# Feed-forward input projections computed by feature, weights as the stationary operand

## The chip, the core and the metric

The kernel runs on one core of a Trainium2 chip. The metric is the device time of the whole launch in microseconds (us). One core has a matrix engine (TensorE, PE in the rows; its weight loads are shown apart as PEld), a vector engine (VectorE, DVE), a scalar engine (ScalarE, ACT), GpSimd (POOL) and a queue engine (SyncE, SP) that issues DMAs. TensorE multiplies a stationary operand of up to 128 x 128 numbers, loaded by a weight load, with a moving operand of up to 512 columns, and adds the result into PSUM. PSUM has eight banks of 512 float32 numbers for each of 128 partitions.

## The reference

Two decoder layers run over 256 tokens of width 2048. Layer 0 mixes tokens by two attention families, layer 1 by a state-space scan. Each layer then has the same feed-forward part, on which the change bears:

```
h = layernorm(alpha * h + mix)
ple = (p[i] @ ple_w[i]) * sigmoid(h @ ple_gate_w[i])
g, u = split(h @ ffn_w_in[i], 2)          # 2048 -> 2 x 5632
h = layernorm(alpha * h + (silu(g) * u) @ ffn_w_out[i] + ple)
```

All is float32. The input projection has 2 x 5632 output features, the output projection maps 5632 features back to 2048.

## The kernel before, in words

**Number format.** Each float32 operand of a large product is split in two numbers of the type float32r, a high part and the rest: `WH` and `WL` for weights (tiles w_hi, w_lo), `XH` and `XL` for activations (x_hi, x_lo), `HH` and `HL` for the hidden features (hid_hi, hid_lo). A product is three matmuls: high with high, high with low, low with high. Activations stand with features on partitions: `XH[:, kt, :]` holds 128 features of all 256 tokens.

**Chunks.** Weights stream in chunks of 256 rows by 512 columns (512 KB). A chunk passes through a ring of four slots: SP loads it to `RAW`, ACT writes `WH` (L712), DVE writes `WL` (L999), TensorE uses both and then counts up `w_used`, which frees the slot. `chunk` (L354 to L364) does one chunk: for each of its two row tiles and each of the two token tiles (128 tokens), three matmuls with the activations stationary (128 x 128) and 512 weight columns moving (L360, L361, L362). That is 12 matmuls of 512 columns and 12 weight loads. The result has tokens on partitions.

**Blocks.** A block is 512 output columns; two PSUM accumulators, each of two banks, alternate between blocks. An input projection block of the feed-forward part takes eight chunks. Its 512 columns are 256 gate features and the 256 matching up features. The hidden width is worked in part A (12 blocks) and part B (10 blocks); after each part comes the output projection over its features (outA with 4 blocks of 12 chunks, outB with 4 blocks of 10 chunks). In both layers together the input projections have 44 blocks, so 352 chunks. The blocks between the first and the last of a part are run by a hardware loop whose body holds two blocks: five passes in part A and four in part B. The function `blocks` writes this loop.

**From accumulator to hidden operand.** While TensorE works on block k, the result of block k-1 is finished. ACT applies Silu to the gate half of both token tiles (`silu`, L877, into `GT[:, 0]`). DVE multiplies by the up half (`hidden`, L1288, into `GT[:, 1]`) and frees the accumulator. TensorE transposes the product (`hidden_turn` calls `turn`, four transposes of 128 x 128, L376) after its fourth chunk of block k, since the output projection needs features on partitions. ACT writes the high part from the transposed PSUM tile (`hidden_hi`, L717) and DVE the rest (`hidden_lo`, L1007). The last block of each part is turned within the first output block.

**What sets the order.** Nothing is scheduled automatically: each engine has its own instruction list, written out in program order, and semaphores with counts tie them (`hid_ready`, `turn_done`, `turned`, `acc_free`, `w_used`, `lo_ready`). `TG` and `HG` number the groups of transposes.

One other place is of use for comparison: the rope key projection (L423 to L425, 48 matmuls) already has weights stationary, 64 columns of them, and 256 token columns moving.

Of the kernel before, what the change touches and what calls it, by code (L numbers as in the profile page):

```python
# [18 lines left out]
F32 = mybir.dt.float32  # L19
F32R = mybir.dt.float32r  # L20
I32 = mybir.dt.int32
ALU = mybir.AluOpType
ACT = mybir.ActivationFunctionType
AX_X = mybir.AxisListType.X

P = 128
# [38 lines left out]
def lin(const, coef=0, i=None):  # L65

    return const if i is None else i * coef + const
# [15 lines left out]
def build(nc, t, out):  # L83
# [3 lines left out]
    with ExitStack() as ctx:  # L87
# [3 lines left out]
        def sem(name):  # L91
            return ctx.enter_context(nc.semaphore(name))
# [105 lines left out]
        ln_act, ln_pool = sem("ln_act"), sem("ln_pool")  # L198

        ple_ready, gate_act, silu_done, hid_ready = sem("ple_ready"), sem("gate_act"), sem("silu_done"), sem("hid_ready")  # L200
        glu_step = sem("glu_step")
        tab, tab_ready, coef_out, ab_turned, ab_ready = sem("tab"), sem("tab_ready"), sem("coef_out"), sem("ab_turned"), sem("ab_ready")
        e_raw = [sem("e_raw0"), sem("e_raw1")]
# [12 lines left out]
        TG = {}  # L216
        n = 0
        for name, count in [("x", 8), ("p0", 1), ("lat", 4), ("qk", 8), ("kpe", 1), ("qn", 4), ("qp", 2), ("kn", 4),
                            ("ln10", 8), ("hid0", FA + FB), ("p1", 1), ("ln11", 8),
                            ("hid1", FA + FB)]:  # L220
            TG[name] = n
            n += count

        HG = {}
        n = 0
        for name, count in [("x", 8), ("p0", 1), ("lat", 4), ("ln10", 8), ("hid0", FA + FB), ("p1", 1), ("ln11", 8),
                            ("hid1", FA + FB)]:
            HG[name] = n
            n += count

# [120 lines left out]
        def _(pe):  # L351
            def chunk(c, coef, i, hi, lo, kt, depth, acc, width=WB):

                pe.wait_ge(lo_ready, lin(c + 1, coef, i))  # L354
                s = c % RING
                for k in range(2):
                    for q in range(TT):
                        cols = slice(q * P, (q + 1) * P)
                        o = A[:, acc, q, 0:width]
                        pe.matmul(o, hi[:, kt + k, cols], WH[:, s, k, 0:width], start=(kt + k == 0), stop=False)  # L360
                        pe.matmul(o, hi[:, kt + k, cols], WL[:, s, k, 0:width], start=False, stop=False)  # L361
                        last = pe.matmul(o, lo[:, kt + k, cols], WH[:, s, k, 0:width], start=False,  # L362
                                         stop=(kt + k == depth - 1))
                last.then_inc(w_used, 1)  # L364

            def acc_ready(b, coef=0, i=None):
# [3 lines left out]
            def turn(g, src, col, coef=0, i=None):  # L370

                if g >= 2:
                    pe.wait_ge(turned, lin(g - 1, coef, i))
                for k in range(2):
                    for q in range(TT):
                        last = pe.transpose(TP[:, g % 2, k, q * P:(q + 1) * P],  # L376
                                            src[:, q, col + k * P:col + (k + 1) * P], ID[:])
                last.then_inc(turn_done, 1)
# [149 lines left out]
            def feed_forward(layer):  # L528
# [46 lines left out]
                            last = pe.matmul(o, BT[:, a, ri, :], CO[:, ri, a, 0:SUB, :], start=(ri == 0), stop=(ri == 1))  # L575
                    last.then_inc(k_done, 1)

                def hidden_turn(b, coef=0, i=None):

                    done = (FA + FB) * layer + b  # L580
                    pe.wait_ge(hid_ready, lin(done + 1, coef, i))
                    turn(TG[f"hid{layer}"] + b, GT[:, 1], 0, coef, i)

                for part, n_in, first in (("A", FA, 0), ("B", FB, FA)):
                    _, per, c0, b0 = PHASES[f"in{part}{layer}"]

                    def inner(k, i):
                        acc_ready(b0 + k, 2, i)
                        for j in range(per):
                            chunk(c0 + per * k + j, 2 * per, i, XH, XL, 2 * j, KT, (b0 + k) % 2)  # L590
                            if j == 3 and k > 0:
                                hidden_turn(first + k - 1, 2, i)
                        if layer == 0 and part == "B" and k == n_in - 1:
                            response(4)
                    blocks(pe, n_in, inner)
                    _, per, c0, b0 = PHASES[f"out{part}{layer}"]
                    for b in range(4):
                        acc_ready(b0 + b)
                        for j in range(per):
                            if b == 0 and j == per - 1:  # L600
                                pe.wait_ge(turned, TG[f"hid{layer}"] + first + n_in)
                            elif b == 0 and j == 0:
                                pe.wait_ge(turned, TG[f"hid{layer}"] + first + n_in - 1)
                            chunk(c0 + per * b + j, 0, None, HH, HL, 2 * j, 2 * n_in, (b0 + b) % 2)
                            if b == 0 and j == 3:
                                hidden_turn(first + n_in - 1)
                        if layer == 0 and (part == "A" or b < 3):
                            response(b if part == "A" else 5 + b)

# [86 lines left out]
        def _(act):  # L696
# [140 lines left out]
            def feed_forward(layer):  # L837
# [31 lines left out]
                def silu(b, coef=0, i=None):  # L869

                    part, k = ("A", b) if b < FA else ("B", b - FA)
                    end(f"in{part}{layer}", k, coef, i)
                    done = (FA + FB) * layer + b
                    if done:
                        act.wait_ge(hid_ready, lin(done, coef, i))
                    parity = (PHASES[f"in{part}{layer}"][3] + k) % 2
                    act.activation(GT[:, 0], A[:, parity, :, 0:256], ACT.Silu).then_inc(silu_done, 1)  # L877

                def hidden_hi(b, coef=0, i=None):
                    k = b if b < FA else b - FA  # L880
                    hi_turned(TG[f"hid{layer}"] + b, HH[:, bass.ds(lin(2 * k, 2 * coef, i), 2), :], coef, i)

                for part, n_in, first in (("A", FA, 0), ("B", FB, FA)):
                    _, per, c0, _ = PHASES[f"in{part}{layer}"]
# [99 lines left out]
        def _(dve):  # L984
# [259 lines left out]
            def feed_forward(layer):  # L1244
# [37 lines left out]
                def hidden(b, coef=0, i=None):  # L1282
                    part, k = ("A", b) if b < FA else ("B", b - FA)
                    bb = PHASES[f"in{part}{layer}"][3] + k
                    done = (FA + FB) * layer + b
                    dve.wait_ge(silu_done, lin(done + 1, coef, i))
                    dve.wait_ge(turn_done, lin(TG[f"hid{layer}"] + b, coef, i))
                    dve.tensor_tensor(GT[:, 1], A[:, bb % 2, :, 256:512], GT[:, 0],  # L1288
                                      ALU.mult).then_inc(hid_ready, 1)

                def hidden_free(b, coef=0, i=None):
                    part, k = ("A", b) if b < FA else ("B", b - FA)
# [4 lines left out]
                def hidden_lo(b, coef=0, i=None):  # L1297
                    k = b if b < FA else b - FA
                    rows = bass.ds(lin(2 * k, 2 * coef, i), 2)
                    lo_turned(TG[f"hid{layer}"] + b, HG[f"hid{layer}"] + b, HH[:, rows, :],  # L1300
                              HL[:, rows, :], coef, i)

                def out_end(part, b, stats):
                    bb = PHASES[f"out{part}{layer}"][3] + b
# [739 lines left out]
```

## Time and profile before

| | |
|---|---|
| median of three runs | 2391.46 us (2389.5 to 2392.58) |
| profiled execution, its own time | 2393.34 us |
| its span, first to last instruction | 2391.5 us |
| mean granted TensorE clock | 0.988 of full speed |
| PE busy | 2316.9 us, 97% of the span |
| PEld busy | 1918.7 us, 80% |
| DVE, ACT, POOL busy | 1450.1, 1022.3, 201.7 us |
| DMA | 478.47 MB, mean 200 GB/s |

The span is what the rows cover; about 1.8 us of the execution's own time lie around it. Busy time counts a matmul from start to modelled end. Matmuls are pipelined, so the mean duration of one (about 390 ns for 512 columns) is longer than the distance to the next start, and it is the distance between starts that tells the rate. A weight load has a row of its own and may run beside the matmul before it.

### The profile page before, as it was taken

The page shows a single profiled execution, that of the slowest core. Times are in us where ns is not written, and L with a number is a line of the kernel's source. Part 1 is how long each engine was busy: PE and PEld are TensorE (multiplying, and loading weights), DVE is VectorE, ACT ScalarE, POOL GpSimd, SP SyncE. Part 2 cuts the span into 40 slices and gives each one's busy share as a digit, 9 for nine tenths or more (in the row PEclk, how much of TensorE's full clock was granted, in tenths as well). Part 3 has the DMA queues.
Part 4 walks back from the last instruction along what each step waited for, and adds up shares of the span by engine and source line. Part 5 has one row for each costly group of instructions (what it writes and reads, how often), then busy time and mean ns, then how long its engine had stood idle before and what let it go on. Part 6 is the DMA issues. An engine that isn't in the chain of part 4 may idle for free.

```text
span 2391.5 us, 34755 instructions
## 1 busy us (share of the span) xinstructions
PE 2316.9 (97%) x12283; PEld 1918.7 (80%) x12283; DVE 1450.1 (61%) x1831; ACT 1022.3 (43%) x1136; POOL 201.7 (8%) x312
## 2 busy tenths in 40 slices
PE   8999999999999999999997799999999999999996
PEld 7888788788888888888886688778888888888885
DVE  5545757666666776556868656665545444545455
ACT  4443544444444334444341544444454433444432
POOL 0000048601111111000100000000000000000000
PEclk9999999999999999999998999999999999999998
DMA  6555254768878777666865356566555555555563
GB/s 235 183 183 160 85 197 156 223 217 263 263 254 259 243 234 237 216 223 205 281 214 177 113 192 190 180 221 194 192 185 192 186 192 193 194 185 192 186 193 114
DMA packets 133881, 478.47 MB, mean 200 GB/s; under 512 B 16144, under 2 KB 17712, under 8 KB 132624
## 3 DMA queue, kind: packets, MB, share of 16 engines
q1 hardware_dynamic: 119280, 427.35, 54.6%
q0 software_dynamic: 13216, 48.20, 6.2%
q8 instruction: 72, 1.18, 0.2%
q10 hardware_dynamic: 1280, 1.48, 0.2%
q14 instruction: 33, 0.27, 0.0%
HBM read 457.82 MB, written 19.14 MB: 199 GB/s over the span
## 4 chain that ended last, share of the span: by engine, by line
PE 94%; DVE 3%; issue 1%; DMA 1%; ACT 1%; SPq 0%; DVEq 0%; ACTq 0%
PE ps L360 29%; PE ps L362 29%; PE ps L361 29%; PE ps L376 1%; PE ps L651 1%; PE ps L664 1%; PE ps L675 1%; DMA raw<-in_w_in 1%; PE ps L386 1%; DVE w_lo L999 0%; PE ps L503 0%; PE ps L575 0%; PE ps L486 0%; PE ps L485 0%; DVE res L1229 0%
## 5 line engine op out<-in xcount | busy, mean ns | idle before, releaser
L999 DVE TENSOR_TENSOR w_lo<-raw,w_hi 128x1024 fp32r<-128x1024 f32 x775 | 951.0, 1230 | 838.3 <-ACT w_hi L712 835.2
L712 ACT ACTIVATE w_hi<-raw 128x1024 fp32r<-128x1024 f32 x775 | 820.5, 1060 | 1165.0 <-PE ps L362 1137.3
L360 PE MATMUL ps<-w_hi,x_hi 128*128 128x512 f32 x2304 | 903.6, 392 | 10.8 <-DVE x_lo L1007 7.2
L362 PE MATMUL ps<-w_hi,x_lo 128*128 128x512 f32 x2304 | 898.0, 390 | 0.0
L361 PE MATMUL ps<-w_lo,x_hi 128*128 128x512 f32 x2304 | 897.4, 390 | 0.0
L360 PEld LDWEIGHTS ps<-w_hi,x_hi 128*128 128x128 f32 x2304 | 432.9, 188 | 101.7 <-DVE x_lo L1007 9.1
L362 PEld LDWEIGHTS ps<-w_hi,x_lo 128*128 128x128 f32 x2304 | 432.9, 188 | 90.8
L361 PEld LDWEIGHTS ps<-w_lo,x_hi 128*128 128x128 f32 x2304 | 433.1, 188 | 88.1
L360 PE MATMUL ps<-w_hi,hid_hi 128*128 128x512 f32 x704 | 275.2, 391 | 0.0
L361 PE MATMUL ps<-w_lo,hid_hi 128*128 128x512 f32 x704 | 274.1, 389 | 0.0
L362 PE MATMUL ps<-w_hi,hid_lo 128*128 128x512 f32 x704 | 273.9, 389 | 0.0
L360 PEld LDWEIGHTS ps<-w_hi,hid_hi 128*128 128x128 f32 x704 | 132.1, 188 | 28.5 <-issue 1.4
L362 PEld LDWEIGHTS ps<-w_hi,hid_lo 128*128 128x128 f32 x704 | 132.2, 188 | 27.7
L361 PEld LDWEIGHTS ps<-w_lo,hid_hi 128*128 128x128 f32 x704 | 132.2, 188 | 27.2
L1761 POOL TENSOR_TENSOR s_small<-s_small 64x128 f32<-64x128 f32 x93 | 70.1, 754 | 7.5
L1882 POOL DMA_DIRECT2D s_e_dram<-s_e x16 | 8.9, 556 | 338.6 <-DVE s_e L1373 338.6
L664 PE MATMUL ps<-u,s_k 32*32 32x64 f32 (+3 forms) x512 | 20.4, 323 | 17.4 <-DVE chain L1657 17.4
L1875 POOL DMA_DIRECT2D s_coef<-s_coef_dram x64 | 35.4, 560 | 5.3 <-DMA s_coef_dram<-s_small 5.3
L1288 DVE TENSOR_TENSOR gated<-ps,gated 128x512 f32<-128x512 f32 x44 | 30.2, 685 | 7.8 <-ACT gated L877 7.8
L664 PEld LDWEIGHTS ps<-u,s_k 32*32 32x32 f32 x512 | 15.5, 115 | 22.3 <-issue 18.7
L1744 POOL DMA_DIRECT2D gb<-in_ln_g x4 | 2.2, 545 | 357.5 <-DVE res L1691 142.2
L675 PE MATMUL ps<-states,s_table 128*32 128x64 f32 x1024 | 19.1, 241 | 12.8 <-issue 12.8
(231 smaller groups left out, 1351.6 us busy)
## 6 DMA issues: line engine op xcount, KB each, us to landing
raw<-in_w_inA SPq DMA_DIRECT2D x192, 512.0 KB, 3.5
raw<-in_w_inB SPq DMA_DIRECT2D x160, 512.0 KB, 3.5
raw<-in_w_outA SPq DMA_DIRECT2D x96, 512.0 KB, 3.5
raw<-in_w_outB SPq DMA_DIRECT2D x80, 512.0 KB, 3.7
raw<-in_w_in SPq DMA_DIRECT2D x64, 512.0 KB, 3.5
raw<-in_w_gate SPq DMA_DIRECT2D x64, 512.0 KB, 4.2
raw<-in_w_glu SPq DMA_DIRECT2D x64, 512.0 KB, 4.2
raw<-in_w_out SPq DMA_DIRECT2D x32, 512.0 KB, 3.5
```

The costliest lines, as they stand in the source:

```text
L360: pe.matmul(o, hi[:, kt + k, cols], WH[:, s, k, 0:width], start=(kt + k == 0), stop=False)
L361: pe.matmul(o, hi[:, kt + k, cols], WL[:, s, k, 0:width], start=False, stop=False)
L362: last = pe.matmul(o, lo[:, kt + k, cols], WH[:, s, k, 0:width], start=False, stop=(kt + k == depth - 1))
L376: last = pe.transpose(TP[:, g % 2, k, q * P:(q + 1) * P], src[:, q, col + k * P:col + (k + 1) * P], ID[:])
L386: pe.matmul(out, ID[:], ID[:], start=True, stop=True)
L664: pe.matmul(outputs(row, a, lag, SUB), KTAB[rows, tile_of(row), lag, :], UT[rows, row, 0:SUB - lag, :].rearrange("p s n -> p (s n)"), star ...
L675: last = pe.matmul(outputs(row, a, s, s + 1), TS[row % 14][:, a, ri, PW * s:PW * (s + 1)], ST[:, row, ri, a, :], start=False, stop=(ri == ...
L712: act.activation(WH[:, s, :, 0:width], RAW[:, s, :, 0:width], ACT.Copy).then_inc(hi_ready, 1)
L999: dve.tensor_tensor(WL[:, s, :, 0:width], RAW[:, s, :, 0:width], WH[:, s, :, 0:width].bitcast(F32), ALU.subtract).then_inc(lo_ready, 1)
L1288: dve.tensor_tensor(GT[:, 1], A[:, bb % 2, :, 256:512], GT[:, 0], ALU.mult).then_inc(hid_ready, 1)
L1761: link(pool.tensor_tensor(o, a, b, op))
L1875: pool.dma_start(EC[n][PW * s:PW * (s + 1)].rearrange("p a c n -> p a (c n)"), src).then_inc(e_raw[n], 16)
```

## The change

In the input projections of the feed-forward part (both layers, parts A and B) the two operands change roles. A new function `chunk_by_feature` takes each 128 x 128 piece of the weight chunk as the stationary operand and moves all 256 tokens past it: for each of two row tiles and four column pieces three matmuls of 256 columns, which makes 24 matmuls and 24 weight loads per chunk. Pieces 0 and 1 (gate features) go to the two halves of the accumulator's first bank, pieces 2 and 3 (up features) to its second. The result has features on partitions. So `silu` reads the first bank and `hidden` the second, `hidden_turn` and its four transposes per block are gone, and `hidden_hi` and `hidden_lo` read the product `GT[:, 1]` itself, no longer the transposed PSUM tile. Two new semaphores, `hid_hi` and `hid_split`, replace the counts of the transposes, and TensorE waits for `hid_split` ahead of the output projection. All else, the chunks' layout and order included, stays.

```diff
+            def chunk_by_feature(c, coef, i, hi, lo, kt, depth, acc):
+
+                pe.wait_ge(lo_ready, lin(c + 1, coef, i))
+                s = c % RING
+                for k in range(2):
+                    for m in range(4):
+                        rows = slice(P * m, P * (m + 1))
+                        o = A[:, acc, m // 2, TOK * (m % 2):TOK * (m % 2 + 1)]
+                        pe.matmul(o, WH[:, s, k, rows], hi[:, kt + k, :], start=(kt + k == 0 and m % 2 == 0), stop=False,
+                                  skip_group_check=True)
+                        pe.matmul(o, WH[:, s, k, rows], lo[:, kt + k, :], start=False, stop=False, skip_group_check=True)
+                        last = pe.matmul(o, WL[:, s, k, rows], hi[:, kt + k, :], start=False, stop=(kt + k == depth - 1),
+                                         skip_group_check=True)
+                last.then_inc(w_used, 1)
...
-                def hidden_turn(b, coef=0, i=None):
-
-                    done = (FA + FB) * layer + b
-                    pe.wait_ge(hid_ready, lin(done + 1, coef, i))
-                    turn(TG[f"hid{layer}"] + b, GT[:, 1], 0, coef, i)
-
...
-                            chunk(c0 + per * k + j, 2 * per, i, XH, XL, 2 * j, KT, (b0 + k) % 2)
-                            if j == 3 and k > 0:
-                                hidden_turn(first + k - 1, 2, i)
+                            chunk_by_feature(c0 + per * k + j, 2 * per, i, XH, XL, 2 * j, KT, (b0 + k) % 2)
...
                             if b == 0 and j == per - 1:
-                                pe.wait_ge(turned, TG[f"hid{layer}"] + first + n_in)
+                                pe.wait_ge(hid_split, (FA + FB) * layer + first + n_in)
                             elif b == 0 and j == 0:
-                                pe.wait_ge(turned, TG[f"hid{layer}"] + first + n_in - 1)
+                                pe.wait_ge(hid_split, (FA + FB) * layer + first + n_in - 1)
                             chunk(c0 + per * b + j, 0, None, HH, HL, 2 * j, 2 * n_in, (b0 + b) % 2)
-                            if b == 0 and j == 3:
-                                hidden_turn(first + n_in - 1)
...
-                    act.activation(GT[:, 0], A[:, parity, :, 0:256], ACT.Silu).then_inc(silu_done, 1)
+                    act.activation(GT[:, 0].rearrange("p t n -> p (t n)"), A[:, parity, 0, :], ACT.Silu).then_inc(silu_done, 1)
...
-                    hi_turned(TG[f"hid{layer}"] + b, HH[:, bass.ds(lin(2 * k, 2 * coef, i), 2), :], coef, i)
+                    act.wait_ge(hid_ready, lin((FA + FB) * layer + b + 1, coef, i))
+                    act.activation(HH[:, bass.ds(lin(2 * k, 2 * coef, i), 2), :], GT[:, 1], ACT.Copy).then_inc(hid_hi, 1)
...
-                    dve.wait_ge(turn_done, lin(TG[f"hid{layer}"] + b, coef, i))
-                    dve.tensor_tensor(GT[:, 1], A[:, bb % 2, :, 256:512], GT[:, 0],
-                                      ALU.mult).then_inc(hid_ready, 1)
+                    if done:
+                        dve.wait_ge(hid_split, lin(done, coef, i))
+                    dve.tensor_tensor(GT[:, 1].rearrange("p t n -> p (t n)"), A[:, bb % 2, 1, :],
+                                      GT[:, 0].rearrange("p t n -> p (t n)"), ALU.mult).then_inc(hid_ready, 1)
...
-                    lo_turned(TG[f"hid{layer}"] + b, HG[f"hid{layer}"] + b, HH[:, rows, :],
-                              HL[:, rows, :], coef, i)
+                    dve.wait_ge(hid_hi, lin((FA + FB) * layer + b + 1, coef, i))
+                    dve.tensor_tensor(HL[:, rows, :], GT[:, 1], HH[:, rows, :].bitcast(F32), ALU.subtract).then_inc(hid_split, 1)
```

TensorE's list before, in the loop of part A of layer 0, between the fourth and the fifth chunk of a block (`gated` is `GT`, `ident` the identity):

```order
2155 L361 MATMUL ps<-w_lo,x_hi 128x512
2156 L362 MATMUL ps<-w_hi,x_lo 128x512
2157 L581 REGISTER_ALU
2158 L373 REGISTER_ALU [waits hid_ready]
2159 L376 MATMUL ps<-ident,gated 128x128 [waits turned]
2160 L376 MATMUL ps<-ident,gated 128x128 x3
2161 L354 REGISTER_ALU
2162 L360 MATMUL ps<-w_hi,x_hi 128x512 [waits lo_ready]
2163 L361 MATMUL ps<-w_lo,x_hi 128x512
2164 L362 MATMUL ps<-w_hi,x_lo 128x512
```

The same place after the change, with the lines of the changed kernel:

```order
2298 L373 MATMUL ps<-x_hi,w_hi 128x256
2299 L375 MATMUL ps<-x_lo,w_hi 128x256
2300 L376 MATMUL ps<-x_hi,w_lo 128x256
2301 L367 REGISTER_ALU
2302 L373 MATMUL ps<-x_hi,w_hi 128x256 [waits lo_ready]
2303 L375 MATMUL ps<-x_lo,w_hi 128x256
2304 L376 MATMUL ps<-x_hi,w_lo 128x256
```

The transposes and TensorE's two waits for them are gone; the chunks follow each other directly, each with twice as many matmuls of half the width.

ACT's list before, in the same loop, at the last chunk of a block:

```order
293 L712 ACTIVATE w_hi<-raw 128x1024 [waits w_used]
294 L716 ISA
295 L717 ISA [waits turn_done]
296 L717 ACTIVATE hid_hi<-ps 128x512
297 L711 REGISTER_ALU [waits raw_full3]
298 L712 ACTIVATE w_hi<-raw 128x1024 [waits w_used]
```

and after:

```order
293 L716 ACTIVATE w_hi<-raw 128x1024 [waits w_used]
294 L885 ISA
295 L886 ISA [waits hid_ready]
296 L886 ACTIVATE hid_hi<-gated 128x512
297 L715 REGISTER_ALU [waits raw_full3]
298 L716 ACTIVATE w_hi<-raw 128x1024 [waits w_used]
```

The high part stands at the same place in ACT's list. It waits for DVE's product instead of TensorE's transposes and reads `GT` instead of PSUM.

## Rows read from the trace of the kernel before

**Rows 1.** The page: busy time by engine, and the granted clock in 40 slices

```profile
PE 2316.9 (97%) x12283; PEld 1918.7 (80%) x12283; DVE 1450.1 (61%) x1831; ACT 1022.3 (43%) x1136; POOL 201.7 (8%) x312
PEclk9999999999999999999998999999999999999998
```

**Rows 2.** The page: the chain that ended last, shares of the span by engine

```profile
PE 94%; DVE 3%; issue 1%; DMA 1%; ACT 1%; SPq 0%; DVEq 0%; ACTq 0%
```

**Rows 3.** Groups by form: count, busy us, mean ns of one, idle before

```profile
L376 PE MATMUL ps<-ident,gated 128*128 128x128 f32 x176 | 26.3, 271 | 0.0
L360 PEld LDWEIGHTS ps<-w_hi,x_hi 128*128 128x128 f32 x2304 | 432.9, 188 | 101.7 <-DVE x_lo L1007 9.1 <-issue 4.3
```

**Rows 4.** Timeline of PE around one turn (start us, us, what)

```profile
1002.37 0.39 PE L361 MATMUL ps<-w_lo,x_hi 128*128 128x512 f32 x1
1002.59 0.39 PE L362 MATMUL ps<-w_hi,x_lo 128*128 128x512 f32 x1
1002.83 0.60 PE L376 MATMUL ps<-ident,gated 128*128 128x128 f32 x4
1003.18 0.48 PE L360 MATMUL ps<-w_hi,x_hi 128*128 128x512 f32 x1
1003.49 0.40 PE L361 MATMUL ps<-w_lo,x_hi 128*128 128x512 f32 x1
1003.73 0.40 PE L362 MATMUL ps<-w_hi,x_lo 128*128 128x512 f32 x1
```

**Rows 5.** Line L376 from 533 to 760 us: durations, first and last start

```profile
L376 PE MATMUL ps<-ident,gated x44: 270/272/273, 533.4 to 756.1; 128*128 128x128 f32 x44
```

**Rows 6.** Line L360 from 1925 to 2000 us, a stretch without transposes

```profile
L360 PE MATMUL ps<-w_hi,hid_hi x110: 389/389/389, 1925.3 to 1999.4; 128*128 128x512 f32 x110
```

**Rows 7.** Line L423, one in three of the rope key's matmuls

```profile
L423 PEld LDWEIGHTS ps<-x_hi,w_hi x16: 134/134/134, 201.5 to 206.7; 128*64 128x64 f32 x16
L423 PE MATMUL ps<-x_hi,w_hi x16: 276/276/281, 201.7 to 206.8; 128*64 128x256 f32 x16
```

**Rows 8.** Lines L651 (64 columns moving) and L386 (one stretch, 128 columns)

```profile
L651 PE MATMUL ps<-u_by_pair,s_table x256: 275/275/294, 1254.2 to 1282.7; 128*128 128x64 f32 x128
L386 PE MATMUL ps<-ident x36: 275/275/275, 1543.8 to 1547.7; 128*128 128x128 f32 x36
```

**Rows 9.** Timelines of PEld and PE where the rope key ends

```profile
206.96 0.13 PEld L425 LDWEIGHTS ps<-x_lo,w_hi 128*64 128x64 f32 x1
207.08 0.19 PEld L360 LDWEIGHTS ps<-w_hi,lat_hi 128*128 128x128 f32 x1
207.07 0.28 PE L425 MATMUL ps<-x_lo,w_hi 128*64 128x256 f32 x1
207.19 0.40 PE L360 MATMUL ps<-w_hi,lat_hi 128*128 128x512 f32 x1
207.42 0.40 PE L361 MATMUL ps<-w_lo,lat_hi 128*128 128x512 f32 x1
207.66 0.39 PE L362 MATMUL ps<-w_hi,lat_lo 128*128 128x512 f32 x1
```

**Rows 10.** Line L362 at 1125.17 us, and the loads around it

```profile
L362 PE MATMUL ps<-w_hi,x_lo x1: 388/388/388, 1125.2 to 1125.2; 128*128 128x512 f32 x1
1124.95 0.19 PEld L362 LDWEIGHTS ps<-w_hi,x_lo 128*128 128x128 f32 x1
1125.49 0.47 PEld L575 LDWEIGHTS ps<-s_c_pow,s_bt 128*32 128x32 f32 x17 [0.35 <-issue]
```

**Rows 11.** Timelines of DVE and ACT within a block of part A, layer 0

```profile
1005.26 0.69 DVE L1007 TENSOR_TENSOR hid_lo<-ps,hid_hi 128x512 f32 x1
1008.55 0.68 DVE L1359 TENSOR_TENSOR s_e<-s_coef,s_b 128x512 f32<-128x512 f32 x1
1018.20 1.23 DVE L999 TENSOR_TENSOR w_lo<-raw,w_hi 128x1024 fp32r<-128x1024 f32 x1 [0.80 <-ACT w_hi L712]
1003.99 0.58 ACT L717 ACTIVATE hid_hi<-ps 128x512 f32 x1
1014.39 1.06 ACT L712 ACTIVATE w_hi<-raw 128x1024 fp32r<-128x1024 f32 x1 [1.66 <-PE ps L362]
```

**Rows 12.** DMA queues from 1664 to 1887 us: packets, MB, share; landing time

```profile
q8 instruction: 2, 0.03, 0.1%
raw<-in_w_inA SPq DMA_DIRECT2D x81, 512.0 KB, 3.4
```

More of the change, by code:

```diff
@@ L200, in build @@
         ple_ready, gate_act, silu_done, hid_ready = sem("ple_ready"), sem("gate_act"), sem("silu_done"), sem("hid_ready")
+        hid_hi, hid_split = sem("hid_hi"), sem("hid_split")
         glu_step = sem("glu_step")
@@ L218, in build @@
         for name, count in [("x", 8), ("p0", 1), ("lat", 4), ("qk", 8), ("kpe", 1), ("qn", 4), ("qp", 2), ("kn", 4),
-                            ("ln10", 8), ("hid0", FA + FB), ("p1", 1), ("ln11", 8),
-                            ("hid1", FA + FB)]:
+                            ("ln10", 8), ("p1", 1), ("ln11", 8)]:
             TG[name] = n
@@ L225, in build @@
         n = 0
-        for name, count in [("x", 8), ("p0", 1), ("lat", 4), ("ln10", 8), ("hid0", FA + FB), ("p1", 1), ("ln11", 8),
-                            ("hid1", FA + FB)]:
+        for name, count in [("x", 8), ("p0", 1), ("lat", 4), ("ln10", 8), ("p1", 1), ("ln11", 8)]:
             HG[name] = n
```

## The prediction

> **What bounds the kernel now.** I read the page's busy times first: PE is busy 97% of the span at a granted clock of full speed in nearly all slices [rows 1], and the chain that ended last is PE for 94% [rows 2]. So only what changes on TensorE counts, unless another engine comes to be waited for. Next I read the rate, from starts and not from durations. In a stretch without transposes one in three 512-column matmuls starts at 1925.3, the 110th at 1999.4: 74.1 us / 109 / 3 = 226.6 ns from start to start [rows 6]. TensorE therefore does a chunk in 12 x 226.6 = 2.72 us. Its weight loads last 188 ns each and lie beside the matmul before them [rows 3, 4]. Last I read the helpers: ACT waits 1.66 us of each 2.72 us for TensorE, and DVE has 0.8 us free even where it has most to do [rows 11].
>
> **What goes: 44 turns.** There are 11 turns of four transposes, one per block, in one stretch [rows 5]; the first transpose starts at 533.4, the last at 756.1. The last of a group starts some 0.3 us after its first (the group lasts 0.60 with 0.27 for one), so ten blocks take 222.4 us, 22.24 each. The 96 matmuls of a block need 96 x 0.2266 = 21.76. A turn thus costs 0.48 us of TensorE's time, more than its 0.44 that are seen at once: from 1002.59 to 1003.49 are 0.90 us where two matmuls would have taken 0.45, and the next ones still follow at 0.23 to 0.24 [rows 4]. 176 transposes are 44 groups [rows 3]. 44 x 0.48 = 21.1 us, all on the path. The transposes' waits had nothing to wait for (idle before them 0.0 [rows 3]), so no stall goes with them.
>
> **What is added: twice the matmuls, each half as wide.** 352 chunks x 24 = 8448 matmuls of 256 columns with 128 x 128 weights, in place of 4224 of 512. Each nanosecond of their spacing is 8.45 us; the even point for the matmuls alone is 113.3 ns, half of 226.6. The trace has no steady stretch of this form. It has each half of it:
> - Moving 256 columns of the same type past 64 columns of weights: 201.7 to 206.8 for 45 matmuls, 113.3 ns [rows 7]. This is exactly half of 226.6, so time goes with moved columns.
> - Loading 128 columns of weights back to back: 28.5 us / 255 = 111.8 ns where only 64 columns move, and 3.9 us / 35 = 111 ns with 128 [rows 8]. The load alone would hold the spacing at that.
> - One single case of both together: the load at 207.08 brings 128 columns while the last 256-column matmul, started at 207.07, runs; the next starts at 207.19 as its peers do, 0.11 to 0.12 later [rows 9].
>
> The two limits, 111.8 and 113.3, lie 1.5 ns apart, and a load starts only when the matmul before it has started. The bounds are then 111.8 (the load alone binds and the moving side's 6% over 2.4 GHz falls away: -12.7 us against 113.3) and 120.1 (below: +57 us). Nearest is the row with 256 columns moving. I take 113.5: +0.2 x 8448 = +1.7 us. After the switch from narrow to wide, matmuls at first follow at 0.23 to 0.24 [rows 9]; there are 4 such switches, at some 0.03 us each: 0.1.
>
> A rule of the Trainium skill speaks against the change. TensorE: Matmul & The Clock Gate, Part 3, says a weight load overlaps matmuls in flight only when its row group differs; here both use all 128 rows. By that rule every pair would be serial. The trace disagrees: the load of 207.08 lies within the matmul of 207.07, and 188 ns loads fit a 226.6 ns spacing with nothing added [rows 6, 9].
>
> **What is moved.** `hidden_hi` and `hidden_lo` keep their places in ACT's and DVE's lists and their sizes; they read SBUF where they read PSUM. For ACT the bounds are 0.58 as now and half of the 1.06 of `w_hi`, which reads SBUF with twice the elements; for DVE 0.69 now and 0.68 for a product with two SBUF operands [rows 11]. I count nothing: the cover is the free time above, and a weight chunk made late by one such operation is still two chunks ahead, since four are in the ring. If that cover were gone, each block would pay up to 0.7 us, 31 us in all. New waits: ACT waits for DVE's product ahead of the high part; behind it in ACT's list stands the next `w_hi`. The product comes after DVE's fifth chunk, the high part at the eighth, so three chunks lie between. TensorE's wait for `hid_split` ahead of the last output chunk of a first block has the same distance as before. Silu and the product have 512 elements per partition in either layout: 0.
>
> **Sum.** Against the profiled execution's own time, 2393.3: -21.1 + 1.7 + 0.1 = -19.3, so 2374.0. That execution stands 1.9 above the median of the runs, so the median to expect is 2372.
>
> **Rivals.**
> - *Loads take time from the moving side (slower).* 226.6 is 13.3 above 512 / 2.4 GHz, and 113.3 is 6.6 above 256 / 2.4 GHz. In both rows the loaded columns are halved too (128 and 64), so the excess may as well go with loaded columns. Then the new form pays 106.7 + 13.3 = 120: 8448 x 6.7 = +57, and the time is 2391.5 - 21.1 + 57 = 2427. For it: both spacings fit, and spacing after a change of form is unsettled, so loads and moving do touch. Against it: the single case of rows 9 (0.12 and no more), and the matmul at 1125.17, which had no load beside it until 1125.49 and still lasts 388 ns, as those with one last 389 [rows 6, 10]. It makes the kernel slower from 113.3 + 21.1 / 8.45 = 115.8 ns upward.
> - *The two near-equal limits jostle.* The unsettled spacing of 0.23 to 0.24 [rows 4, 9] is 115 to 118 for a half. Lasting, this gives 2384 to 2410, centre 2395.
> - *The loop's code no longer stays in TensorE.* From 1664 to 1887, five passes of the loop, only 2 packets of code were fetched [rows 12], so a body of 200 matmuls stayed. The new one has 384. If it did not stay, each of the 14 jumps back (4 + 3 per layer) could wait for a transfer. The nearest price is a weight chunk's landing, 3.4 us [rows 12]: up to 48, so 2371 + 48 = 2419 at most, less what TensorE has queued. The Trainium skill (Runtime: NRT & Kernel Launch, Instruction fetch mechanics) gives PE room for 2048 instructions and warns of jumps out of the window; by that figure a body of some 790 stays. No row here shows the room.
> - *Pairs are serial.* Load and matmul one after the other: 111.8 + 113.3 = 225 ns, 8448 x 112 = +946, 3316. This is what the skill's rule above would give; rows 9 speak against it.
> - *Loads alone bind.* 111.8: 2372 - 14 = 2358. Against it: rows 7 have a lighter load and keep 113.3.
> - *The gain is given back.* The turns' 21 us turn into waits of TensorE for the accumulator or for `hid_split`: 2391. Against it: no idle time ahead of TensorE in these parts today [rows 3].
>
> **How the numbers follow.** Forecast 0.66 (own range 2367 to 2380); jostling 0.10; loads taking time 0.14; code fetched 0.04; serial 0.01; loads alone 0.03; given back 0.02. A change under 0.2%, 4.8 us, can't be told from none. Faster: forecast, loads alone and a third of jostling, 0.72. Same: 0.06, from jostling and the gain given back. Slower: 0.22. The range starts at 2366, under which only 'loads alone' lies, and reaches into the slower cases to 2412 (118.2 ns); what is left out is 'loads alone', 'serial', the upper end of the code case and most of 'loads taking time', together some 2 in 10.
>
> **What would show it.** PE's starts within an input block: 113 to 114 ns apart, 2.72 us per chunk, 21.8 per block; `ident,gated` transposes gone; no idle time of PE ahead of the input matmuls or of the first output block; code packets absent from most of the loop's time; ACT's and DVE's operations at 0.55 to 0.6 and 0.68. A spacing of 115.8 or more, or a gap of microseconds at each second block, would make the prediction wrong.

## The result, and the profile after

| | before | after |
|---|---|---|
| median | 2392.02 us (2389.5 to 2394.59) | 2425.68 us (2423.01 to 2426.71) |
| ratio | | 1.0142, 95% interval 1.0129 to 1.0154 |
| span of the profiled execution | 2391.5 us | 2423.4 us |

The kernel became 33.7 us slower. Predicted were 2372 us and a range up to 2412: the time lies above the range, and the change went the other way than forecast. It lies where the rival "loads take time from the moving side" put it (2427), to which I had given 0.14.

The profile's page of the changed kernel, to be read against [rows 1, 2, 3]: busy times, the granted clock, the chain's shares, and the groups of the new matmuls.

```profile
span 2423.4 us, 42730 instructions
PE 2346.4 (97%) x16331; PEld 2118.1 (87%) x16331; DVE 1448.1 (60%) x1831; ACT 1023.7 (42%) x1136; POOL 203.8 (8%) x312
PEclk9999999999999999999998999999999999999998
PE 94%; DVE 3%; issue 1%; ACT 1%; DMA 1%; SPq 0%; DVEq 0%; ACTq 0%
L373 PE MATMUL ps<-x_hi,w_hi 128*128 128x256 f32 x2816 | 797.1, 283 | 0.0
L375 PE MATMUL ps<-x_lo,w_hi 128*128 128x256 f32 x2816 | 796.9, 283 | 0.0
```

TensorE is still the bound, the clock is granted as before, DVE and ACT are as busy as before, and no idle time stands ahead of the new matmuls. So the time was not lost in waits; it must lie in the matmuls' own rate. The duration (283 ns) is not that rate, since one matmul starts before the last has ended. The starts give it. TensorE's timeline in the loop of part A of layer 1, first its matmuls, then its weight loads:

```profile
1699.82 0.28 PE L373 MATMUL ps<-x_hi,w_hi 128*128 128x256 f32 x1
1699.94 0.28 PE L375 MATMUL ps<-x_lo,w_hi 128*128 128x256 f32 x1
1700.06 0.28 PE L376 MATMUL ps<-x_hi,w_lo 128*128 128x256 f32 x1
1700.18 0.28 PE L373 MATMUL ps<-x_hi,w_hi 128*128 128x256 f32 x1
```

```profile
1699.82 0.19 PEld L375 LDWEIGHTS ps<-x_lo,w_hi 128*128 128x128 f32 x1
1699.94 0.19 PEld L376 LDWEIGHTS ps<-x_hi,w_lo 128*128 128x128 f32 x1
1700.06 0.19 PEld L373 LDWEIGHTS ps<-x_hi,w_hi 128*128 128x128 f32 x1
```

The starts are 0.12 us apart, and each load starts with the matmul before it. One line's matmuls over 200 us of the same loop (first and last start, count) make it exact:

```profile
L373 PE MATMUL ps<-x_hi,w_hi x557: 283/283/283, 1699.8 to 1900.0; 128*128 128x256 f32 x186
```

200.2 us / 556 / 3 = 120.0 ns, where I had taken 113.5. A chunk takes 24 x 120.0 = 2.88 us and not 2.72, a block 23.04 and not the 22.24 of before with its turn.

**The account.** 8448 matmuls x 6.67 ns (120.0 less the 113.33 of before for as many columns) = +56.3 us, less the turns' 21.1, is +35.2. The traces agree: from the first matmul of one phase to the first of the next, the four input phases are 10.0, 8.4, 10.0 and 8.4 us longer than before, and the three output projections that are not beside the scan 0.45 us shorter each, the turn that they held. The spans differ by only 31.9. The 3.3 between the two lies in stretches that the change doesn't touch. In two of them the profiled execution was granted a higher clock than that of before; that this is all of the 3.3 is not shown. The windows of both kernels, before and then after: the chunks of the start, and the scan between the layers (columns: stretch, its length, then PE, PEld, DVE, ACT and POOL busy with counts, the granted clock, DMA share, GB/s).

```profile
17.00:30.00 13.00, 11.04 (x48) 8.75 (x47) 6.61 (x7) 5.46 (x7) 0.00 (x0) 0.87 0.74 265
1300.00:1345.00 45.00, 34.39 (x1315) 28.44 (x1315) 44.04 (x147) 20.44 (x29) 0.00 (x0) 0.89 0.20 63
```

```profile
17.00:30.00 13.00, 11.27 (x56) 9.09 (x55) 7.38 (x9) 7.01 (x9) 0.00 (x0) 1.00 0.78 265
1315.50:1360.50 45.00, 33.27 (x1352) 27.76 (x1353) 44.13 (x147) 20.73 (x29) 0.00 (x0) 0.93 0.20 64
```

### The profile page after: what moved, and what is told of

Read it like the earlier page. It is cut to its first block, busy times and chain, and to the rows that moved or that the text cites. A ratio compares the mean times of both kernels' runs of the same rounds, so it can differ in the third digit from the quotient of the medians.

```text
span 2423.4 us, 42730 instructions
## 1 busy us (share of the span) xinstructions
PE 2346.4 (97%) x16331; PEld 2118.1 (87%) x16331; DVE 1448.1 (60%) x1831; ACT 1023.7 (42%) x1136; POOL 203.8 (8%) x312
## 4 chain that ended last, share of the span: by engine, by line
PE 94%; DVE 3%; issue 1%; ACT 1%; DMA 1%; SPq 0%; DVEq 0%; ACTq 0%
PE ps L359 16%; PE ps L361 15%; PE ps L360 15%; PE ps L373 14%; PE ps L375 14%; PE ps L376 14%; PE ps L655 1%; PE ps L668 1%; PE ps L679 1%; PE ps L400 1%; DMA raw<-in_w_in 1%; PE ps L390 1%; DVE w_lo L1004 0%; PE ps L517 0%; PE ps L589 0%
## 5 line engine op out<-in xcount | busy, mean ns | idle before, releaser
L373 PE MATMUL ps<-x_hi,w_hi 128*128 128x256 f32 x2816 | 797.1, 283 | 0.0
L375 PE MATMUL ps<-x_lo,w_hi 128*128 128x256 f32 x2816 | 796.9, 283 | 0.0
L376 PE MATMUL ps<-x_hi,w_lo 128*128 128x256 f32 x2816 | 796.9, 283 | 0.0
L373 PEld LDWEIGHTS ps<-x_hi,w_hi 128*128 128x128 f32 x2816 | 540.6, 192 | 0.3 <-issue 0.2
L375 PEld LDWEIGHTS ps<-x_lo,w_hi 128*128 128x128 f32 x2816 | 540.7, 192 | 0.1
L376 PEld LDWEIGHTS ps<-x_hi,w_lo 128*128 128x128 f32 x2816 | 540.7, 192 | 0.0
L359 PE MATMUL ps<-w_hi,x_hi 128*128 128x512 f32 x896 | 351.6, 392 | 11.3 <-DVE x_lo L1012 7.3
L361 PE MATMUL ps<-w_hi,x_lo 128*128 128x512 f32 x896 | 349.6, 390 | 0.0
L360 PE MATMUL ps<-w_lo,x_hi 128*128 128x512 f32 x896 | 349.3, 390 | 0.0
L360 PE MATMUL ps<-w_lo,hid_hi 128*128 128x512 f32 x704 | 274.1, 389 | 0.0
L360 PEld LDWEIGHTS ps<-w_lo,x_hi 128*128 128x128 f32 x896 | 168.6, 188 | 34.3
L360 PEld LDWEIGHTS ps<-w_lo,hid_hi 128*128 128x128 f32 x704 | 132.2, 188 | 27.1
```

The lines of the kernel that those rows point to most:

```text
L373: pe.matmul(o, WH[:, s, k, rows], hi[:, kt + k, :], start=(kt + k == 0 and m % 2 == 0), stop=False, skip_group_check=True)
L375: pe.matmul(o, WH[:, s, k, rows], lo[:, kt + k, :], start=False, stop=False, skip_group_check=True)
L376: last = pe.matmul(o, WL[:, s, k, rows], hi[:, kt + k, :], start=False, stop=(kt + k == depth - 1), skip_group_check=True)
```

## The experiments

**1. Matmul forms alone.** A kernel of its own with 15 series of 48 matmuls, each with its own weight load, and a last one in which the types alternate; nothing else runs beside them. It leaves out the whole computation.

```
for k in range(N):                                            # N = 48
    pe.matmul(o(0, 512), w(k, 128), XR[:, 512:1024], ...)     # 128 loaded, 512 moved
for k in range(N):
    pe.matmul(o(1, 384), w(k, 128), XR[:, 0:384], ...)        # then 320, 256, 128 moved
...
for k in range(N):
    pe.matmul(o(1, 512, 64), w(k, 64), XR[:, 0:512], ...)     # 64 loaded; then 32, 96
...
```

> A kernel of its own that leaves out the whole computation: stretches of 48 matmuls of one form each on random data, no other engine at work meanwhile. Theory A (loads take time from the moving side): spacing = moved columns / 2.4 GHz + 13.3 ns x loaded columns / 128. So for moved/loaded 512/128 226.7, 384/128 173.3, 320/128 146.7, 256/128 120.0, 512/64 220.0, 256/64 113.3, 512/32 216.7, 256/32 110.0, 256/96 116.7 ns. Theory B (two limits side by side: the moving side at 0.4427 ns per column, a load of 128 columns beside it at 120 ns, the later one sets the spacing): 226.7, 170.0, 141.7, 120.0, 226.7, 113.3, 226.7, 113.3, and 113.3 for 256/96. Theory C (traffic of ACT, DVE and DMA slows TensorE's reads): 512/128 falls to 216 and 256/128 to 112 here. Reloading the same weights each time: 120.0 by A and B. bfloat16 operands and the mix of two float32r matmuls and one bfloat16 are open: if the excess belongs to the 4-byte loads, bfloat16 at 512/128 comes to about 216.

The timeline's rows (start, time from the first start to the last end). A form such as 128*64 128x512 is 128 rows by 64 loaded columns, and 512 moved.

```profile
23.53 11.04 PE L61 MATMUL ps<-x_round,w_round 128*128 128x512 f32 x48
34.41 8.51 PE L63 MATMUL ps<-x_round,w_round 128*128 128x384 f32 x48
42.76 7.19 PE L65 MATMUL ps<-x_round,w_round 128*128 128x320 f32 x48
49.79 5.92 PE L67 MATMUL ps<-x_round,w_round 128*128 128x256 f32 x48
55.54 5.48 PE L69 MATMUL ps<-x_round,w_round 128*128 128x128 f32 x48
60.85 11.21 PE L71 MATMUL ps<-x_round,w_round 128*64 128x512 f32 x48
71.90 5.63 PE L73 MATMUL ps<-x_round,w_round 128*64 128x256 f32 x48
99.50 5.91 PE L81 MATMUL ps<-x_round,w_round 128*128 128x256 f32 x48
105.25 10.53 PE L83 MATMUL ps<-x_bf,w_bf 128*128 128x512 bf16 x48
115.62 5.40 PE L85 MATMUL ps<-x_bf,w_bf 128*128 128x256 bf16 x48
```

The time less the duration of one, over 47, is the mean spacing. The first few matmuls of a series still follow the form before them, so the table gives the spacing of the settled second half, which differs from that mean by at most 0.8 ns. The granted clock was 1.00 throughout the series of the table.

| loaded, moved | spacing, ns | above moved / 2.4 GHz |
|---|---|---|
| 128, 512 | 226.6 | 13.3 |
| 128, 384 | 173.3 | 13.3 |
| 128, 320 | 146.7 | 13.4 |
| 128, 256 | 120.0 | 13.3 |
| 128, 256, the same weights each time | 120.0 | 13.3 |
| 128, 128 | 111.6 | 58.3 |
| 96, 256 | 116.0 | 9.3 |
| 64, 256 | 113.3 | 6.6 |
| 32, 256 | 113.3 | 6.6 |
| 64, 512 | 230 | 17 |
| 32, 512 | 232 | 18 |
| bfloat16: 128, 512 | 215.9 | 2.5 |
| bfloat16: 128, 256 | 109.2 | 2.5 |

With 128 columns loaded in float32r the excess is 13.3 ns a matmul at 256, 320, 384 and 512 moved columns; with 128 moved the spacing is 111.6, what a load alone seems to take. The 120.0 and 226.6 stand with all other engines idle: traffic has no part in it. Both of my theories fell in part, though. The excess is not in proportion to what is moved, but nor is it in proportion to what is loaded: lighter loads help at 256 moved columns and do harm at 512.

**2. More forms, and both types mixed** (again without the computation).

> A kernel of its own that leaves out the whole computation, as the first one with other forms. With 128 loaded columns the first one showed an excess of 13.3 ns per matmul over moved columns / 2.4 GHz, whatever was moved (256 to 512), and 111.6 ns where 128 were moved. Theory A' (a fixed 13.3 ns per matmul with a full load, floor 111.7): 288 gives 133.3, 240 gives 113.3, 192 gives 111.7 ns. Theory B (0.4427 ns per moved column or the load at 120): 127.5, 120, 120. With fewer loaded columns the excess was 6.7 at 256 moved and 16.7 at 512: by an excess per moved column it is 5.8 at 448, or 10.0 at 384 and 8.3 at 320 by a straight line through 6.7 and 16.7 it is 11.7 and 9.2; I expect no clean rule. Groups of 4 float32r and 8 bfloat16 matmuls of 512: 4 x 226.7 + 8 x 215.8 + 24 for the two switches = 2657 ns, if only a switch costs; 8 and 4: 2701 ns; 8 and 16 of 256 moved: 8 x 120 + 16 x 109.2 + 24 = 2731 ns.

```profile
23.96 6.48 PE L61 MATMUL ps<-x_round,w_round 128*128 128x288 f32 x48
35.65 5.50 PE L65 MATMUL ps<-x_round,w_round 128*128 128x192 f32 x48
50.70 8.48 PE L69 MATMUL ps<-x_round,w_round 128*64 128x384 f32 x48
98.83 1.28 PE L80 MATMUL ps<-x_round,w_round 128*128 128x512 f32 x4
101.50 1.28 PE L80 MATMUL ps<-x_round,w_round 128*128 128x512 f32 x4
```

288 columns took 131.6 ns a matmul, 11.6 above 2.4 GHz, so 13.3 is not exact for every width; 240 and 192 took 112.0 and 111.6, near the 111.6 of experiment 1. With 64 loaded columns 384 took 173.3, as with 128; with 96 loaded, 512 took 230, as with 64. So the excess with narrow loads follows no law that I can state. Of the mixtures, four float32r and then eight bfloat16 matmuls of 512 columns repeat every 2.67 us, 2.72 for twelve in float32r; eight and four took 2.73, no less than all in float32r. Eight and sixteen of 256 columns took 2.71, in place of 24 x 0.12 = 2.88:

```profile
161.07 1.19 PE L90 MATMUL ps<-x_round,w_round 128*128 128x256 f32 x8
163.78 1.20 PE L90 MATMUL ps<-x_round,w_round 128*128 128x256 f32 x8
```

**3. No turns, operands as before.** The changed kernel with `chunk` in place of `chunk_by_feature`. Silu and the product read the accumulator as before. The transposes are left out, so the hidden features are not turned and the output is not the reference's.

```diff
-                            chunk_by_feature(c0 + per * k + j, ...)
+                            chunk(c0 + per * k + j, ...)
...
-                    act.activation(..., A[:, parity, 0, :], ACT.Silu).then_inc(silu_done, 1)
+                    act.activation(GT[:, 0], A[:, parity, :, 0:256], ACT.Silu).then_inc(silu_done, 1)
```

> The kernel before with the transposes left out (the hidden product goes to the output projection with tokens where features should be; the matmuls of the input projections are those of before). My sum: 44 turns x 0.48 us = 21.1 us less than before, 2371. If turns cost only what a timeline shows between neighbours (0.44): 2372.6. If the waits that replace them bite: 2392 as before.

2368.08 us against 2389.53, ratio 0.991 (0.9894 to 0.9927): the turns cost 21.4 us (17 to 25 by the interval), 21.1 were predicted, and the rest of the change (helpers from SBUF, new waits) nothing that shows. It is 57.6 us faster than the changed kernel was, 55.1 when each is taken against the kernel before that ran beside it, and 8448 x 6.67 is 56.3. The loss is the matmuls' form, within that noise all of it.

**4. Half the weights loaded.** The changed kernel with 64 of each 128 columns stationary; half of the features are not computed.

```diff
-                        rows = slice(P * m, P * (m + 1))
-                        o = A[:, acc, m // 2, ...]
+                        rows = slice(P * m, P * m + P // 2)
+                        o = A[0:P // 2, acc, m // 2, ...]
```

> The changed kernel with only the first 64 of each 128 weight columns made stationary (half of the features left out of the projection), still 24 matmuls of 256 moved columns per chunk. Both theories A and B: spacing 113.3 ns instead of 120.0, so 8448 x 6.7 = 56 us less than the changed kernel, 2369. If the spacing comes from the 256 moved columns or the two half banks written, it stays 120 and 2426.

```profile
L373 PE MATMUL ps<-x_hi,w_hi x530: 276/276/276, 1699.9 to 1879.8; 128*64 128x256 f32 x177
```

179.9 / 529 / 3 = 113.4 ns, and 2367.94 us, one execution. With as many matmuls and as many moved columns the whole loss is gone, in the kernel itself. The loaded columns are also the output's partitions (64 in place of 128), so this run does not part the load from the writing of the result.

**5. The kernel before with its matmuls halved.** Activations stationary and turns kept; each matmul of 512 columns is done as two of 256.

```diff
+                        for m in range(2):
+                            part = slice(TOK * m, TOK * (m + 1))
+                            o = A[:, acc, q, part]
+                            pe.matmul(o, hi[:, kt + k, cols], WH[:, s, k, part], ...)
+                            pe.matmul(o, hi[:, kt + k, cols], WL[:, s, k, part], ...)
+                            last = pe.matmul(o, lo[:, kt + k, cols], WH[:, s, k, part], ...)
```

> The kernel before, with each 512-column matmul of the input projections done as two of 256 columns on the same stationary activations, the transposes kept. If only the count of loads matters and not which operand is stationary: spacing 120.0, 8448 x 6.67 = 56 us more than before, 2448. If the weights as the stationary operand are what is slow (their place, or the piece layout): spacing 113.3 and 2392.

```profile
L376 PE MATMUL ps<-w_hi,x_hi x491: 280/283/365, 1699.9 to 1879.7; 128*128 128x256 f32 x164
```

179.8 / 490 / 3 = 122.3 ns, the turns among them (one per 192 matmuls, 0.48 us each, 2.5 ns a matmul): 120 without. One execution took 2443.46 us, 53.9 above the median of before beside it, where 56 were expected. Which operand holds does not matter; the number of matmuls does.

**6. Another order.** The changed kernel with the low weights' matmul second and the low activations' third, so that `w_hi` is not loaded twice in a row.

> The changed kernel with the second and the third matmul of each piece exchanged, so that no two matmuls in a row have the same stationary weights. If a load is done for every matmul in any case: the time of the changed kernel, 2426. If the repeated weights make the second load cheaper today: slower, up to 120 ns instead of 113.3 for one in three less whatever it saves, so over 2430.

2425.7 us, ratio 1.015 (1.0133 to 1.0167), the same as the changed kernel. Loading what is loaded already costs as much as loading something new, as the row with the same weights in experiment 1 says: the weights are "held" in name only, and there are 24 loads per chunk.

**7 and 8. The low-order terms in bfloat16, the kernel before otherwise.** The mixture of experiment 2 in the whole kernel: `w_lo` and `x_lo` are written as bfloat16, and copies of `w_hi` and `x_hi` in bfloat16 beside them, `w_hi`'s by DVE in 7 and by ACT in 8, `x_hi`'s by DVE in both. The low-order terms then keep bfloat16's precision. A chunk does its four float32r matmuls first and then its eight of bfloat16.

```diff
+                for k in range(2):
+                    for q in range(TT):
+                        cols = slice(q * P, (q + 1) * P)
+                        pe.matmul(A[:, acc, q, 0:width], hi[:, kt + k, cols], WH[:, s, k, 0:width], ...)
                 for k in range(2):
                     for q in range(TT):
...
-                        pe.matmul(o, hi[:, kt + k, cols], WH[:, s, k, 0:width], ...)
-                        pe.matmul(o, hi[:, kt + k, cols], WL[:, s, k, 0:width], ...)
-                        last = pe.matmul(o, lo[:, kt + k, cols], WH[:, s, k, 0:width], ...)
+                        pe.matmul(o, hb[:, kt + k, cols], WL[:, s, k, 0:width], ...)
+                        last = pe.matmul(o, lo[:, kt + k, cols], WB16[:, s, k, 0:width], ...)
... 7, DVE, behind w_lo:
+                dve.tensor_copy(WB16[:, s, :, 0:width], WH[:, s, :, 0:width].bitcast(F32)).then_inc(lo_ready, 1)
... 8, ACT, behind w_hi:
+                act.activation(WB16[:, s, :, 0:width], RAW[:, s, :, 0:width], ACT.Copy).then_inc(whb_ready, 1)
```

> The kernel before (tokens on partitions, turns kept), with the two low-order terms of every product in bfloat16: w_lo and x_lo are written as bfloat16, and DVE writes bfloat16 copies of w_hi and x_hi behind its lo products. A chunk is 4 float32r matmuls of 512 columns and then 8 bfloat16 ones; in the second run of matmul forms such a group took 2.67 us in place of 2.72. If TensorE still sets the rate, 774 chunks save 0.05 us each, 38.7 us: 2353. Rival: the copies fill DVE (1450 us busy plus 774 x about 1 us is 2224 or more of 2392), TensorE waits for w_lo where DVE has other work, and the time is above 2392.

> The same matmuls, but ACT writes the bfloat16 copy of w_hi from the raw chunk (a second activation of about 1.06 us per chunk); DVE keeps only the copies of x_hi. ACT goes from 1022 us busy to about 1840, DVE stays near 1450 to 1520. If TensorE sets the rate: 2353 as above. Rival: ACT's two activations (2.12 us) and its share of the block's end leave it less than 2.67 us per chunk, TensorE waits at block ends, and some of the 38.7 us is lost: 2360 to 2400.

With the copy on DVE: 2383.6 us, ratio 0.9974 (0.9965 to 0.9984), between the 2353 expected and the rival's 2392 and more. On ACT: 2361.68 us, ratio 0.9882 (0.9866 to 0.9899), 28.0 us faster. The busy times and the shares of the chain of waits, first with the copy on DVE, then on ACT:

```profile
PE 2270.4 (95%) x12087; PEld 1295.7 (54%) x12283; DVE 1941.7 (82%) x2704; ACT 1019.8 (43%) x1136; POOL 228.5 (10%) x312
PE 80%; DVE 12%; issue 4%; DMA 2%; ACT 1%; POOL 0%; SPq 0%; DVEq 0%; ACTq 0%
```

```profile
PE 2265.4 (96%) x12087; PEld 1299.0 (55%) x12283; DVE 1487.4 (63%) x1929; ACT 1746.9 (74%) x1911; POOL 203.7 (9%) x312
PE 92%; DVE 4%; issue 2%; ACT 2%; DMA 1%; SPq 0%; DVEq 0%; ACTq 0%
```

And TensorE's waits (line, what it waited for: us in total, times, longest), in the same order:

```profile
PE ps L365 <- DVE w_hi_bf L1012: 17.9, 24, 3.6
PE ps L365 <- DVE x_hi_bf L1020: 13.5, 8, 2.7
```

```profile
PE ps L369 <- DVE x_hi_bf L1025: 12.2, 8, 2.5
PE ps L369 <- DVE w_lo L1016: 6.4, 3, 3.1
```

The same matmuls differ by 22 us through the engine that feeds them: with the copies on DVE the chain of waits runs through DVE for 12%, and TensorE waits 24 times for the copy. The copy took 0.70 us and `w_lo`, now written as bfloat16, 1.23. On ACT a chunk takes 2.67 us, as in experiment 2. 10.7 us are missing to the expected 38.7. The traces show two stretches in which this kernel is the slower one: around the first gate block of layer 0, and around the per-layer embedding (`ple`) and first gate block of layer 1, where TensorE takes each x tile as soon as DVE has made it. The same stretches, between the first matmuls of the same chunks, before and then with the copy on ACT (columns as above):

```profile
397.60:428.60 31.00, 27.75 (x153) 23.05 (x151) 26.34 (x31) 12.42 (x17) 27.77 (x41) 1.00 0.43 134
1521.80:1571.90 50.10, 43.13 (x214) 35.48 (x212) 33.16 (x54) 22.61 (x28) 1.05 (x2) 0.97 0.43 150
```

```profile
390.20:425.50 35.30, 29.17 (x153) 18.18 (x153) 29.62 (x38) 19.30 (x25) 31.49 (x48) 0.95 0.36 120
1498.40:1554.60 56.20, 44.71 (x211) 25.46 (x212) 35.59 (x61) 34.20 (x41) 1.05 (x2) 0.94 0.42 144
```

They are 4.3 and 6.1 us longer. TensorE waits longer there for the x tiles (12.2 us in all, 7.2 before), and its granted clock is lower (0.95 and 0.94, for 1.00 and 0.97).

**9. The change and bfloat16 together.** The changed kernel, with the low-order terms as in 8.

```diff
+                for k, m in pieces:
...
+                    pe.matmul(o, WH[:, s, k, P * m:P * (m + 1)], hi[:, kt + k, :], ...)
+                for k, m in pieces:
...
+                    pe.matmul(o, WB16[:, s, k, rows], lo[:, kt + k, :], ...)
+                    last = pe.matmul(o, WL[:, s, k, rows], hb[:, kt + k, :], ...)
```

> The changed kernel (features on partitions, no turns) with the low-order terms in bfloat16 and ACT writing the bfloat16 copy of w_hi, as in the run e8. An input chunk is then 8 float32r matmuls of 256 columns and 16 in bfloat16; in the second run of matmul forms such a group took 2.72 us, as a chunk of the kernel before does, so the 44 x 0.48 = 21.1 us of the turns would be kept; the other 422 chunks save 0.05 us each, 21.1. Together 2392 - 42 = 2350, less what e8 lost of its 38.7 (it gained 28): 2350 to 2361, about as e8. Rival: the excess of narrow matmuls stays 13.3 ns in this mixture too, a chunk takes 2.88 us, and the time is 2361.7 + 56 - 21 + 18 = about 2405 to 2415.

The timeline of input blocks (a row holds the eight float32r matmuls of a chunk; the last row shown is the tenth after the first):

```profile
1700.79 1.19 PE L386 MATMUL ps<-x_hi,w_hi 128*128 128x256 f32 x8
1703.50 1.20 PE L386 MATMUL ps<-x_hi,w_hi 128*128 128x256 f32 x8
...
1727.92 1.19 PE L386 MATMUL ps<-x_hi,w_hi 128*128 128x256 f32 x8
```

27.13 us for ten chunks, 2.71 each. The time is 2357.49 us against 2392.22, ratio 0.9859 (0.9842 to 0.9875): 34.7 us faster than the kernel before beside it, and the best of all. Against experiment 8 it is 4.2 us faster by the medians, 6.7 when each is taken against its own kernel before. The change pays here, but by little: halving the matmuls still costs 2.71 in place of 2.67 us a chunk, which takes back most of what the turns give. In the loop of part A of layer 1 a block takes 21.71 us, and 21.79 with its turn in experiment 8; 44 x 0.09 = 3.8 us.

## Why the prediction was wrong

- **The step that failed** is the price of the new matmul: "Nearest is the row with 256 columns moving. I take 113.5: +0.2 x 8448 = +1.7 us." It measured 120.0 ns and +56.3 us, the bound of 120.1 that I had written beside it. This one term turns -19.3 into +35.3.
- **Why I chose badly.** Rows 6 and 7 differ in two things at once, moved columns (512, 256) and loaded columns (128, 64). Their ratio of exactly 2 I read as "time goes with moved columns". It was an accident of two excesses, 13.3 and 6.6 ns. The text of the rival said so, and I weighed it down with one single case [rows 9]: "0.11 to 0.12 later". That reading, to 0.01 us, could not tell 113 from 120, and finer it would have misled: the trace has 114 ns there. It was one matmul at the end of a series with narrow weights and no steady state; the three after it followed at 232, 236 and 228 ns. That the loads "fit a 226.6 ns spacing with nothing added" passed over the 13.3 ns that were in it.
- **The other argument against it** was the matmul at 1125.17, as long without a load beside it as with one [rows 10]. A duration is no second witness beside the spacing: in every series of the table it is 160 to 164 ns more than the spacing (276 and 283 ns for 113.4 and 120.0 in experiment 4 and the changed kernel). So the 388 ns say that this matmul carried the same excess with no load beside it, as far as a modelled end can say it. That speaks against the rival's mechanism, not against its price, and I took it for the price.
- **Right:** the turns (21.1 predicted, 21.4 measured in experiment 3); helpers and new waits at nothing. `hidden_hi` grew from 0.58 us to 0.615, which its cover hid; `hidden_lo` took 0.685. The group of `hidden_hi` after the change (minimum, median and maximum of one in ns):

```profile
L886 ACT ACTIVATE hid_hi<-gated x44: 611/615/617, 534.5 to 2306.6; 128x512 f32 x36, 128x512 fp32r<-128x512 f32 x8
```

- **The rivals.** Loads taking time from the moving side: right in the time (2427 for 2425.68), and with half the columns loaded the loss is gone (experiment 4); but not as the law it assumed, for the excess does not go with loaded columns at 512 moved (experiment 1). Jostling limits: no; the spacing is steady at 120.0. Serial pairs, 225 ns: no, a load starts with the matmul before it and the pair takes 120. The Trainium skill (TensorE: Matmul & The Clock Gate, Part 3) says that a load overlaps running matmuls only when its row group differs; this trace does not agree, since both use all 128 rows. Loads alone, 111.8: not at 256 columns; the spacing is that with 240 or fewer. The gain given back: no, experiment 3 keeps 21.4 us of it. Code fetched: between 1735 and 1920 us, in the loop, the queue shows only weights, and TensorE is busy for all 185 us. The DMA queue of that stretch:

```profile
q1 hardware_dynamic: 9225, 33.59, 61.1%
```

- **What stays open:** what the 13.3 ns are. The runs show that they come with each float32r matmul that has a full load, hardly with bfloat16 ones (2.5), and that a narrower load does not always lower them. In no run did a float32r matmul go without a load of its own, so they can't part the load's share from the matmul's own. Bfloat16 differs in both: its loads last 98 ns, those of float32r 188 to 192.

## What to carry to other kernels

Count matmuls and not only columns: with float32r each one with a full load cost 13.3 ns beside its columns, so two of 256 cost 6% more than one of 512, and that outweighed the removal of a turn (four transposes, 0.48 us) per 96 matmuls. Before a form is priced by a ratio of two rows, look for everything in which the rows differ; where two things changed together, give the alternative the weight that its bound has, or measure the form alone. And ask which of the products need the dear type: the same exchange of operands lost 34 us in float32r and gained 4 to 7 us with the low-order terms in bfloat16.

## What the runs showed of the hardware

- At a granted clock of 1.00 a float32r matmul with 128 loaded columns follows the last after moved / 2.4 GHz + 13.3 ns with 256, 320, 384 and 512 columns, after 131.6 ns with 288, and after 111.6 to 112.0 with 240, 192 and 128; a bfloat16 one after moved / 2.4 GHz + 2.5 ns with 256 and 512.
- Loading 64 or 32 columns in place of 128 made 256 moved columns faster (113.3 for 120.0 ns) and 512 slower (230 and 232 for 226.6).
- The same weights loaded again cost what new ones do (120.0 ns).
- A change of type between neighbours of 512 columns costs something: float32r, bfloat16, float32r in turn took 0.69 us per three, where their spacings add to 0.67; four and then eight took 2.67 us, where they add to 2.63, and eight and four 2.73 for 2.68. With 256 columns, eight and sixteen, nothing shows: 2.71 for 2.71.
- DVE's lo product took 1.23 us with bfloat16 output; the plain copy of float32 to bfloat16 in SBUF took 0.70 on DVE and 1.04 on ACT.
